# Turning the attention weights by half tiles of 64 rows, with four score banks and GpSimd's sums moved

## The reference

```
q, k, v      = projections of rms_norm(x)          # heads of 64
o_a          = gates * (compressed, selected and window attention)   # 4 heads
o_b          = causal attention over latents         # 4 heads, 96 columns of q and k
o_c          = banded attention, 128 keys back, with sinks            # 8 heads
p            = softmax(q @ k^T * scale + bias)       # per block of 128 queries
o            = p @ v
mixed        = concat(o_a, o_b, o_c) * silu(z)
x            = x + rms_norm(mixed @ w_out, g_post)
```

## Time and profile before

| | |
|---|---|
| time, median of 3 runs | 1317.56 us (1317.01 to 1317.94) |
| the profiled execution | 1317.59 us |
| its span | 1315.8 us |
| TensorE busy | 1269.0 us, 96% |
| VectorE busy | 694.2 us, 53% |
| ScalarE busy | 416.9 us, 32% |
| GpSimd busy | 395.7 us, 30% |
| DMA | 96.59 MB, mean 73 GB/s |
| mean granted clock of TensorE | 0.995 of full speed |

### The profile page before, as it was taken

How to read it: one execution, slowest core, us unless ns; L and a number is a source line. 1 busy time by engine, 2 the same in 40 slices (tenths; PEclk the granted TensorE clock), 3 DMA queues, 4 the chain that set the end, 5 groups by cost and what they waited for, 6 DMA issues and landing times.

```text
span 1315.8 us, 24615 instructions
## 1 busy us (share of the span) xinstructions
PE 1269.0 (96%) x9971; PEld 773.3 (59%) x9971; DVE 694.2 (53%) x1422; ACT 416.9 (32%) x904; POOL 395.7 (30%) x470
## 2 busy tenths in 40 slices
PE   5999999999999999999999999998999999999997
PEld 3454555555656676686445885455645786446653
DVE  4356667847234444574463653257646374237735
ACT  4244213263433322110033003246613112236721
POOL 0100000202334443182432320138631240128731
PEclk9999999999999999999999999999999999999999
DMA  9710112101230200042415315110004415100001
GB/s 312 283 64 2 64 65 80 36 29 65 74 122 3 67 3 3 2 174 83 164 56 136 96 33 192 64 53 1 2 16 102 131 33 192 65 1 2 1 1 64
DMA packets 71536, 96.59 MB, mean 73 GB/s; under 512 B 27640, under 2 KB 35248, under 8 KB 71423
## 3 DMA queue, kind: packets, MB, share of 16 engines
q1 hardware_dynamic: 71050, 94.76, 21.7%
q10 hardware_dynamic: 372, 0.27, 0.1%
HBM read 92.89 MB, written 2.13 MB: 72 GB/s over the span
## 4 chain that ended last, share of the span: by engine, by line
PE 84%; DVE 5%; SPq 3%; POOL 3%; ACT 2%; issue 1%; DMA 1%; POOLq 0%; DVEq 0%; ACTq 0%
PE PS L147 80%; PE PS L2830 2%; POOL AR L3117 1%; SPq L187 1%; POOL AR L2053 1%; DVE AR L2936 1%; DMA bias_rows<-AR 1%; DMA AR<-in_final_g 1%; SPq L308 1%; SPq L304 0%; SPq L309 0%; ACT AR L3058 0%; SPq L312 0%; POOL AR L3115 0%; DVE AR L2923 0%
## 5 line engine op out<-in xcount | busy, mean ns | idle before, releaser
L147 PE MATMUL PS<-AR 64*64 64x64 f32 (+13 forms) x9334 | 1196.1, 326 | 20.9 <-ACT AR L3068 5.4
L147 PEld LDWEIGHTS PS<-AR 64*64 64x64 f32 (+5 forms) x9334 | 703.0, 152 | 483.8 <-issue 385.5
L3058 ACT ACTIVATE AR<-AR 128x257 f32<-128x257 f32 (+5 forms) x160 | 84.9, 530 | 99.0 <-DVE AR L2936 89.6
L2936 DVE CUSTOM_DVE_ANT_0 AR<-PS,AR 128x257 f32<-128x257 f32 (+5 forms) x160 | 72.3, 452 | 61.7 <-PE PS L147 44.4
L412 POOL TENSOR_TENSOR AR<-AR 128x1 f32<-128x1 f32 (+4 forms) x26 | 21.9, 841 | 258.0 <-DVE AR L407 211.3
L1189 DVE SCALAR_TENSOR_TENSOR AR<-AR 128x441 f32<-128x441 f32 (+2 forms) x96 | 78.6, 819 | 15.7 <-ACT AR L1146 12.0
L3117 POOL TENSOR_SCALAR AR<-AR 128x257 f32<-128x257 f32 (+5 forms) x96 | 53.4, 557 | 59.4 <-DVE AR L2942 52.0
L1612 DVE TENSOR_TENSOR AR<-PS,AR 128x256 f32<-128x256 f32 x60 | 25.5, 425 | 85.7 <-PE PS L147 82.3
L3115 POOL TENSOR_SCALAR AR<-AR 128x128 f32<-128x128 f32 (+3 forms) x64 | 38.9, 608 | 63.0 <-DVE AR L2942 58.3
L2053 POOL TENSOR_TENSOR AR<-AR 128x512 f32<-128x512 f32 x36 | 47.7, 1324 | 28.5 <-DMA AR<-in_w_o 25.5
L2830 PE MATMUL PS<-AR 128*128 128x128 f32 x352 | 50.8, 282 | 5.1 <-DVE AR L2923 3.4
(11 more groups left out here) (264 smaller groups left out, 956.4 us busy)
## 6 DMA issues: line engine op xcount, KB each, us to landing
AR<-in_w_in SPq DMA_DIRECT2D x16, 2048.0 KB, 9.1
AR<-in_w_mod SPq DMA_DIRECT2D x6, 2048.0 KB, 13.0
AR<-in_w_out SPq DMA_DIRECT2D x4, 2048.0 KB, 12.7
AR<-in_x SPq DMA_DIRECT2D x8, 512.0 KB, 5.2
AR<-in_w_in SPq DMA_DIRECT2D x4, 1024.0 KB, 7.4
AR<-in_w_o SPq DMA_DIRECT2D x2, 2048.0 KB, 8.0
AR<-in_w_in SPq DMA_DIRECT2D x2, 1664.0 KB, 8.7
AR<-in_w_in SPq DMA_DIRECT2D x12, 256.0 KB, 4.2
```

The costliest lines, as they stand in the source:

```text
L147: return t.matmul(o, l, r, start=s, stop=p, skip_group_check=True)
L2936: v.do.tensor_tensor_reduce(PB[j % NJP][e][:, 0:nk], ps["s", l, j, e][:, 0:nk], bias_for(qb, kind, 2 * a + e, nk), 1.0, 3e38, ALU.add, ALU ...
L3058: a_.do.activation(P, P, ACT.Exp, bias=mn[:, j % NJS, e:e + 1], scale=-1.0, accum_out=su[:, j % NJS, e:e + 1]).then_inc(sa, na("p", l, j, e))
```

## The change

Behind the gate tiles (jobs 9 to 39, `by_halves`) a block is turned in two halves of 64 query rows, `turn_halves`. The half r of every block of both heads goes to bank 3 + r, and the halves alternate. One semaphore count stands for the whole job, and both banks are taken at once. VectorE and ScalarE then copy by halves of the queries where they copied by heads, and the products read the turned weights with the queries in two pieces. The scores rotate over four banks (2, 5, 0, 1). From iteration 13 on the order on TensorE, VectorE and ScalarE is another one. GpSimd's first six differences move to the wide jobs of the last query block, the other six and the factor `pst` behind the loop.

```diff
+    TURNED = 3
+    def by_halves(j):
+        return j > FILLED - TURN
+    def turns_first(i):
+        return (i <= FILLED) == (i % 2 == 0)
...
         few = itertools.cycle((0, 1)), itertools.cycle((3, 4))
-        all_ = itertools.cycle((2, 0, 1)), itertools.cycle((5, 3, 4))
+        all_ = (itertools.cycle((2, 5, 0, 1)),)
...
+        def turn_halves(j):
+            qb, kind, a = JOBS[j]
+            k0, nb, nk, at = keys_of(qb, kind)
+            p = ps.take_two(t, "pT", l, j, bank=TURNED)
+            for e in range(2):
+                t.wait_ge(sg, ng["normed", l, j, e])
+                for b in range(nb):
+                    for r in range(2):
+                        c = 512 * r + 64 * (nb * e + b)
+                        x = t.go.transpose(p[:, c:c + 64], PB[j % NJP][e][64 * r:64 * r + 64, at[b]:at[b] + 128],
+                                           ident[64 * r:64 * r + 64, 64 * r:64 * r + 64])
+            x.then_inc(st, nt("pT", l, j))
...
-                    x = mm(t.go, o[64 * e:64 * e + 64, c], vv, PT[j % NJT][:, e, 128 * b:128 * b + 128],
-                           b == 0 and kind != "win", b == nb - 1)
+                    oo, pp = o[64 * e:64 * e + 64, c], PT[j % NJT][:, e, 128 * b:128 * b + 128]
+                    if by_halves(j):
+                        oo, pp = oo.rearrange("p (r x) -> p r x", r=2), PT[j % NJT][:, :, 64 * (nb * e + b):64 * (nb * e + b) + 64]
+                    x = mm(t.go, oo, vv, pp, b == 0 and kind != "win", b == nb - 1)
...
-            if i % 2 == 0:
+            if i <= FILLED and i % 2 == 0:
                 turned(i), filled(i), scored(i), summed(i)
+            elif i <= FILLED:
+                summed(i), scored(i), filled(i), turned(i)
+            elif i % 2 == 0:
+                scored(i), turned(i), summed(i)
             else:
-                summed(i), scored(i), filled(i), turned(i)
+                summed(i), turned(i), scored(i)
...
-        e_.wait_ge(st, nt["pT", l, j, e])
+        e_.wait_ge(st, nt[("pT", l, j) if by_halves(j) else ("pT", l, j, e)])
...
+        if by_halves(j):
+            src, dst = ps.two("pT", l, j).rearrange("p (r n) -> p r n", r=2), PT[j % NJT]
+            src, dst = (x[:, :, 0:w_] if e == "both" else x[:, e, 0:w_] for x in (src, dst))
...
@@ attn_v
-            if i % 2 == 0:
+            if turns_first(i):
                 turned(i)
...
-            if i % 2:
+            if not turns_first(i):
                 turned(i)
...
@@ attn_a
-            if i % 2 == 0:
+            if i > FILLED or turns_first(i):
                 turned(i)
             if i < NJ:
                 expo(i)
-            if i % 2:
+            if i <= FILLED and not turns_first(i):
                 turned(i)
...
@@ attn_g
+        SUMS = [i for i in range(3 * PER, NJ) if JOBS[i][1] != "swa"]
...
+            if i == SUMS[0]:
+                g.wait_ge(st, nt["sz", l, 3])
...
-            if 14 <= i < 38 and i % 2 == 0:
-                if i == 14:
-                    g.wait_ge(st, nt["sz", l, 3])
-                sums_of_weights(g, w0 + 8, w0 + 9, ("y2", l), (i - 14) // 2)
-            if i == 15:
-                g.wait_ge(s_pst, 16 * (l + 1))
-                g.do.tensor_scalar(pst, pst, 32.0, None, ALU.mult).then_inc(sg, ng("pst", l))
+            if i in SUMS:
+                sums_of_weights(g, w0 + 8, w0 + 9, ("y2", l), SUMS.index(i))
+        for i in range(len(SUMS), 12):
+            sums_of_weights(g, w0 + 8, w0 + 9, ("y2", l), i)
+        g.wait_ge(s_pst, 16 * (l + 1))
+        g.do.tensor_scalar(pst, pst, 32.0, None, ALU.mult).then_inc(sg, ng("pst", l))
```

More of the change, by code:

```diff
@@ L2868, in turned @@
             if TURN <= i < NJ + TURN:
-                turn(i - TURN)
+                (turn_halves if by_halves(i - TURN) else turn)(i - TURN)
             if qb < 4 and at == CMP_TURN:
@@ L2918, in out_of_psum @@
         p = ps["pT", l, j, e]
-        if e == "both":
+        if by_halves(j):
+            src, dst = ps.two("pT", l, j).rearrange("p (r n) -> p r n", r=2), PT[j % NJT]
+            src, dst = (x[:, :, 0:w_] if e == "both" else x[:, e, 0:w_] for x in (src, dst))
+        elif e == "both":
             src, dst = p.rearrange("p (e n) -> p e n", e=2)[:, :, 0:w_], PT[j % NJT][:, :, 0:w_]
@@ L2923, in out_of_psum @@
         write(dst, src).then_inc(sem, count("pT", l, j, e))
-        ps.empty(sem, count, "pT", l, j, e)
+        ps.empty(sem, count, *(("pT", l, j) if by_halves(j) else ("pT", l, j, e)))
     def attn_v(v, l):
@@ L2934, in least @@
                 if j >= NJP:
-                    v.wait_ge(st, nt["pT", l, j - NJP, "both" if narrow(j - NJP) else e])
+                    o = j - NJP
+                    v.wait_ge(st, nt["pT", l, o] if by_halves(o) else nt["pT", l, o, "both" if narrow(o) else e])
                 v.do.tensor_tensor_reduce(PB[j % NJP][e][:, 0:nk], ps["s", l, j, e][:, 0:nk], bias_for(qb, kind, 2 * a + e, nk), 1.0, 3e38,
```

## The result

The changed kernel takes 1325.25 us (median of 4 runs, 1323.77 to 1325.83) against 1317.5 us for the one before on the same chip: ratio 1.0058, 95% interval 1.0046 to 1.0069. It is 7.75 us slower, where 1314.8 us was forecast, and lies above the range of 1308.0 to 1321.0. The profiled execution took 1325.83 us, its span is 1324.0 us. The first thing to read is the granted clock of TensorE, a mean of 0.982 in place of 0.995; the four runs lie at 0.982 to 0.986.

The account below looks back on a forecast made before the run. VectorE, about 90% occupied, was taken to bound the long attention pieces, TensorE only the tail. Two layers of -1.0 (bubble) and -0.4 (tail) made -2.8 us on 1317.59: 1314.8 us, range 1308.0 to 1321.0.

Parts of the forecast that it names:

- TensorE's relief "at nothing": Long attention piece: 7.4 us from half tiles and 3 from order, hidden behind VectorE; up to 10 us per layer without cover.
- rival (c): Wide jobs: TensorE with less to do is throttled again, two stretches of 3.0 us each, 1320.8 us; chance 0.05.
- The bubble: VectorE's wait around the odd turn: 0.48 us a pair, 6.2 us in place of 7.2, -1.0 per layer.
- Rival (b): Single pair of turn banks ties TensorE to VectorE's queue: 0.8 us a pair, +2.8 per layer, 1323.2 us; chance 0.12.
- the whole long piece: Attention from job 13's first score to job 39's score, 71.1 us in layer 0; forecast -1.0 us per layer.
- queued behind it on TensorE are the next scores: Odd iteration's turn waits for the even one's copy, holding up scores VectorE needs; 0.23 to 0.48 us bubble on VectorE.
- rival (d): Row halves don't overlap: a block costs 0.124 us, +3 to +6 per layer, about 1323 us; chance 0.03.
- the forecast's 7.4 us a layer: Blocks turned behind the gate tiles: half tiles relieve TensorE of 7.4 us per layer, bounds 2.7 and 7.4.
- The tail: Stretch without scores before the closing product, where TensorE alone sets the end: -0.4 us per layer, bounds -1.3 and +0.3.
- GpSimd: Moved sums and factor end at 962 us, hidden with 6 us to spare; earlier waits already counted in the 7.2 us.
- The signs: If right: TensorE's busy time well below 63 us, VectorE waits 5 to 7 us, half tiles 0.03 us, GpSimd done near 962.
- the signs against: If wrong: VectorE waiting under 4 or over 9 us, clock 0.50 among wide jobs, or closing product waiting for GpSimd.

Follow-up runs that it names:

- e5: Changed kernel plus an unread dense TensorE product before each odd iteration's turn (512 columns until job 19, 256 behind it); 1320.19 us, ratio 1.001 to the kernel before.
- e1: Kernel before with only GpSimd's part of the change, its sums and norm factor moved later; 1314.91 us, ratio 0.9978.
- e4: Changed kernel with odd iterations' scores moved ahead of the turn that waits for the copy; 1310.97 us, ratio 0.9948 to the kernel before.
- e3: Changed kernel with whole 128x128 blocks turned again, new order and banks kept; 1329.87 us, ratio 1.0089 to the kernel before.
- e8: Changed kernel with odd iterations' scores ahead of the turn and whole 128x128 blocks turned; 1313.91 us, ratio 0.9972 to the kernel before.
- e2: Changed kernel with odd gated jobs' scores computed an extra, unread time before the turn; 1323.23 us, ratio 1.0047 to the kernel before.

## Why the prediction was wrong, point by point

**The step that failed** is the one that costed TensorE's relief "at nothing" behind VectorE's work, and the chance of 0.05 given to rival (c), the clock. Its stretch in layer 1 before was read as "it cost nothing visible", and from that the narrow jobs were left out of rival (c) altogether. Of the two it is the clock that cost the time. The mechanism was seen and its price was nearly right: 0.44 us for each us at half the clock (3.0 of 6.8) against 0.51 and 0.37 measured among wide jobs. The amount was wrong: not two stretches of 6.8 us but 17.1, 10.2 and 10.2 us. The sum from rows: the narrow jobs took 22.02 and 20.37 us, and with the clock held by e5's filler 18.15 and 17.80, which makes 3.9 and 2.6; the wide jobs of layer 1 took 3.8 more than those of layer 0. Together 10.3 us. The profiled execution less these is 1325.83 - 10.3 = 1315.5 us, 0.7 us from the forecast and as long as e1 (1315.33 profiled). That nearness is in part luck, as the paragraph on GpSimd says.

**The bubble** was not what failed. At full clock, in the jobs 20 to 39 of layer 0, VectorE waited 4.0 us for ten pairs, 0.40 a pair where 0.48 was taken.

**Why the same clock cost nothing before.** The narrow jobs of layer 1 before took 18.08 us at a clock of 0.81, those of layer 0 18.44 at 1.00: TensorE was busy 17.48 us in place of 15.61 and filled its own waits. Layer 1 is that much quicker at full clock too (e1: 17.48 and 17.14 us), so the stretch cost nothing. With three turn banks no turn waited over 0.9 us for VectorE's copy. After, the chain copy, half tiles, scores, minimum goes once around both engines, so what TensorE loses can be added on VectorE; the one place shown above is the wait of 3.01 us.

**Why the clock fell.** TensorE's waits for the copy grew to 10.7 us, and the third fall, at 1242.37 us, came behind 6.4 us in which it was busy 3.98: the end of one wait for VectorE's copy, of 1.60 us until 1236.36, and one of 2.05 us until 1242.39. But the same two waits stand in layer 0 in the fence below on half tiles, and the clock stayed up there; and ahead of the first fall, at 877.14 us, there is one wait for the copy alone, of 0.84 us. What is shown is what brings more half clock or less: scores ahead of the waiting turn and whole blocks each take away about half of it, both together all of it (e4, e3, e8), and e5's filler kept it out of the narrow jobs. That is read from one profiled execution of each; the mean clocks of the other runs go the same way (0.982 to 0.986 after the change, 0.990 to 0.991 with whole blocks, 0.989 to 0.996 with the scores first, 0.994 to 0.997 with both). Which idle time of TensorE brings a fall, and why one execution of a program has a stretch and the next has none (e4's 0.989 and 0.996), is open.
The Trainium skill has this case in "TensorE: Matmul & The Clock Gate", section "A second HAM failure mode: psum-queue depth-cycling": a kernel that cycles through PSUM banks can leave TensorE idle for short gaps so often that its clock goes down and up. The trace agrees so far: ten waits of 1.1 us in the mean for one pair of banks, none above 2.1 us, and 17.1 us at half the clock in the same stage. It doesn't show which of them did it.

**Rival (b), the single pair at any clock,** was in the game too. It alone would have been 1323.2. At full clock the order and the pair cost 0.9 and 1.5 us in the middle and wide piece (e3 against e1), and half tiles gave 1.3 and 1.4 back, so the two cancelled: jobs 20 to 39 of layer 0 took 52.1 us against 52.8 before, -0.7 (-1.0 was forecast for the whole long piece), of which GpSimd's part is 0.4. Moving the scores ahead of the waiting turn, the sentence "queued behind it on TensorE are the next scores" read as an instruction, was worth 14.3 us with what the clock gave back, and 1.4 us in each of the last two pieces of a layer at full clock. That gain stood in no rival.

**Half tiles.** Eight took from 919.88 to 920.18 us and sixteen from 931.64 to 932.24:

```profile
919.88 0.46 PE L2840 MATMUL PS<-AR 64*128 64x64 f32 x8 [0.42 <-DVE AR L2955]
920.18 2.10 PE L147 MATMUL PS<-AR 64*128 64x257 f32 x12
...
929.58 0.46 PE L2840 MATMUL PS<-AR 64*128 64x64 f32 x8 [1.60 <-DVE AR L2955]
...
931.64 0.67 PE L2840 MATMUL PS<-AR 64*128 64x64 f32 x16
932.24 1.32 PE L147 MATMUL PS<-AR 128*64 128x128 f32 x20
...
935.61 0.59 PE L2840 MATMUL PS<-AR 64*128 64x64 f32 x12 [2.05 <-DVE AR L2955]
```

Sixteen last 0.67 us less some 0.22 for the last record: 15 steps of 0.030 us, and a block costs 0.060 where 0.062 was taken. Row halves do overlap; rival (d) is out. Up to the next shape a half tile takes 0.0375 us (0.60 for sixteen), a block 0.075, where ten whole blocks took 0.124 each in the same way (923.08 to 924.32 us in the earlier trace rows). By either measure the saving is near the forecast's 7.4 us a layer. So this term was right too.

**The tail** was to give 0.4 us and gave nothing: 8.39 us behind job 39's minimum in both. Half tiles gave 1.1 there (e3 takes 9.47 with whole blocks), and order and single pair took 1.1 (e3 against the 8.39 before), where 0.85 was forecast.

**GpSimd** was forecast at no gain of its own beyond VectorE's waits, and 6 us away from who needs it. It ended at 967.1 us, 5 us later than the 962 forecast, and 5.2 us before VectorE's first use of the factor at 972.3:

```profile
954.88 9.00 POOL L2053 TENSOR_TENSOR AR<-AR 128x512 f32<-128x512 f32 x6
964.04 3.02 POOL L3172 TENSOR_SCALAR AR<-AR 128x1024 f32<-128x1024 f32 x1 [0.17 <-POOL AR L2053]
```

Nobody waited, so that reading was right. Its gain was booked inside the bubble's sum, where 1.0 us of VectorE's waiting did go. But that gain is 2.9 us in all (e1), as much as the whole forecast of -2.8. So half tiles, order and banks together gave nothing at full clock, and that the sum of the rows above comes near the forecast is luck to that extent.

**The signs** named ahead: TensorE's busy time fell at full clock, half tiles at 0.030 us, the product's wait for ScalarE gone and nobody waiting for GpSimd came as said; GpSimd's end near 962 us and VectorE's waits of 5 to 7 us did not. Of the signs against, two came: VectorE waiting over 9 us (10.6) and a clock of 0.50 among wide jobs. The rule of the Trainium skill weighed in the prediction ("TensorEngine Tiling (Array Packing)", PSUM Bottleneck: the emptying of PSUM may become the limit) fits the kernel after at full clock: TensorE's work fell by 5.6 us in jobs 20 to 39 of layer 0, the time by 0.7. But the emptying wasn't the whole limit: with the same copies and minima on VectorE, e4's order took another 1.4 us off each of the two pieces.

## What to carry to other kernels

Work taken from TensorE where another engine sets the pace isn't free: look at where its new idle time falls, and price a stretch at half the clock (here 0.37 to 0.55 us a us where the engines are tied), above all if the trace of before already shows one there. When a buffer is taken away, put everything that doesn't need it ahead of the instruction that now waits for it; here that order was worth 14 us, and with it and whole blocks the buffer's loss cost nothing (0.9972 for e8, 0.9978 for e1, each against the kernel before). And cut stages at the pacing engine's instructions, not at those of one that runs ahead through its buffers.

## What the runs showed of the hardware that was not expected

The granted clock of one program differs from run to run and moves its time: 1319.1 to 1328.4 us at 0.993 to 0.987 (e2), 1308.5 to 1313.8 at 0.996 to 0.989 (e4), while the kernel before kept to 0.993 to 0.998 and 1316.9 to 1319.2 us in all executions but the one named above. A stretch at half the clock can cost nothing (6.8 us in layer 1 before, where VectorE set the pace) or half its length (3.4 of 6.8 us in e4). With less work on TensorE the clock was lower in the order of the change: 0.990 to 0.991 with whole blocks, 0.982 to 0.986 with half tiles, four runs each.
